# Gated activations and their token sums, 64 bytes further on

## What is computed

```python
def _conv_ffn(x, w_up, conv_w, conv_b, w_down):
    S = x.shape[1]
    h = x @ w_up
    hp = jnp.pad(h, ((0, 0), (CONV_WIDTH - 1, 0), (0, 0)))
    hc = conv_b + sum(conv_w[kk] * hp[:, kk:kk + S] for kk in range(CONV_WIDTH))
    gate = hc[..., :D_FF]
    up = hc[..., D_FF:]
    return (jax.nn.silu(gate) * up) @ w_down
```

## Time and profile before

| | us |
|---|---|
| median of three runs | 2093.48 |
| lowest and highest run | 2093.47, 2095.21 |
| the profiled execution | 2093.4 |
| its span, first to last instruction | 2091.6 |
| TensorE busy | 2083.9 |
| VectorE busy | 1526.0 |
| ScalarE busy | 1226.9 |

### The profile page before, as it was taken

One profiled execution on the slowest core, in us unless ns is written; L12 is line 12 of the kernel. 1 busy time (PEld: TensorE's weight loads), 2 busy tenths in 40 slices (PEclk: granted clock), 3 DMA queues, 4 the chain that ended last, 5 costly groups with the idle time before them and its releaser, 6 DMA issues.

```text
span 2091.6 us, 38907 instructions
## 1 busy us (share of the span) xinstructions
PE 2083.9 (100%) x14540; PEld 1923.5 (92%) x14540; DVE 1526.0 (73%) x2707; ACT 1226.9 (59%) x2223; POOL 2.7 (0%) x12
## 2 busy tenths in 40 slices
PE   9999999999999999999999999999999999999999
PEld 9999889999999998888788888899999999988887
DVE  5767777767676679888756558667766676688888
ACT  5655566555565555666656666566555565555654
POOL 0000000000000000000000000000000000000000
PEclk9999999999999999999999999999999999999999
DMA  9655666555655555556554454745555656555554
GB/s 351 236 170 166 215 214 216 189 193 181 201 199 191 190 181 201 201 182 226 185 171 151 167 187 161 256 157 192 201 192 189 200 180 201 177 204 182 201 201 161
DMA packets 201631, 408.97 MB, mean 196 GB/s; under 512 B 7616, under 2 KB 9152, under 8 KB 200768
## 3 DMA queue, kind: packets, MB, share of 16 engines
q1 hardware_dynamic: 201392, 407.45, 57.4%
q10 hardware_dynamic: 144, 0.26, 0.0%
HBM read 404.53 MB, written 3.15 MB: 195 GB/s over the span
## 4 chain that ended last, share of the span: by engine, by line
PE 98%; DVE 1%; ACT 0%; issue 0%
PE acc L1771 32%; PE acc L1769 32%; PE acc L1770 32%; PE acc L2091 0%; PE acc L1968 0%; PE acc L2065 0%; PE acc L1882 0%; PE acc L1949 0%; PE acc L1934 0%; PE acc L2115 0%; PE acc L1875 0%; PE acc L2123 0%; DVE x_tok L1740 0%; DVE next_w_lo L1058 0%; PE acc L1994 0%; PE acc L1961 0%
## 5 line engine op out<-in xcount | busy, mean ns | idle before, releaser
L1058 DVE TENSOR_TENSOR w_lo<-raw,w_hi 128x512 fp32r<-128x512 f32 x1326 | 878.3, 686 | 410.5 <-ACT w_hi L626 405.9
L626 ACT ACTIVATE w_hi<-raw 128x512 fp32r<-128x512 f32 x1326 | 809.2, 630 | 541.3 <-PE acc L1771 528.1
L1769 PE MATMUL acc<-ffn_xT,w_hi 128*128 128x256 f32 x2920 | 806.9, 276 | 0.0
L1770 PE MATMUL acc<-ffn_xT,w_hi 128*128 128x256 f32 x2920 | 806.0, 276 | 0.0
L1771 PE MATMUL acc<-ffn_xT,w_lo 128*128 128x256 f32 x2920 | 806.0, 276 | 0.0
L1770 PEld LDWEIGHTS acc<-ffn_xT,w_hi 128*128 128x128 f32 x2920 | 548.2, 188 | 0.2
L1769 PEld LDWEIGHTS acc<-ffn_xT,w_hi 128*128 128x128 f32 x2920 | 548.2, 188 | 0.2
L1771 PEld LDWEIGHTS acc<-ffn_xT,w_lo 128*128 128x128 f32 x2920 | 548.1, 188 | 0.0
L1770 PE MATMUL acc<-w_lo,ffn_act 128*128 128x512 f32 (+1 forms) x640 | 234.0, 366 | 0.0
L1769 PE MATMUL acc<-w_hi,ffn_act 128*128 128x512 f32 (+1 forms) x640 | 233.9, 365 | 0.0
L1771 PE MATMUL acc<-w_hi,ffn_act 128*128 128x512 f32 (+1 forms) x640 | 233.7, 365 | 0.0
(11 more groups left out here) (294 smaller groups left out, 1975.9 us busy)
## 6 DMA issues: line engine op xcount, KB each, us to landing
raw<-in_ffn_w_up SPq DMA_DIRECT2D x172, 1024.0 KB, 5.0
raw<-in_ffn_w_down SPq DMA_DIRECT2D x88, 1024.0 KB, 5.1
raw<-in_diff_w_in SPq DMA_DIRECT2D x38, 1024.0 KB, 5.7
raw<-in_w_out SPq DMA_DIRECT2D x32, 1024.0 KB, 5.1
raw<-in_pool_w_in SPq DMA_DIRECT2D x16, 1024.0 KB, 5.2
raw<-in_mem_w_kv SPq DMA_DIRECT2D x12, 1024.0 KB, 12.4
next_from_raw<-in_ffn_w_up SPq DMA_DIRECT2D x4, 1024.0 KB, 9.8
head_first<-in_first SPq DMA_DIRECT2D x5, 768.0 KB, 11.1
```

The lines of the kernel that those rows point to most:

```text
L626: nc.scalar.activation(hi, raw_place(st, c, k, j), ACT.Copy).then_inc(hi_made, 1)
L1058: nc.vector.tensor_tensor(lo, raw_place(st, c, k, j), hi.bitcast(F32), ALU.subtract).then_inc(lo_made, 1)
L1769: pe.matmul(out, w[0], x[0], start=start, stop=False, skip_group_check=True)
L1770: pe.matmul(out, w[0], x[1], start=False, stop=False, skip_group_check=True)
```

## The change

The tile act and the tile pair_x start 64 bytes further on: the margin before them is 32 floats instead of 16, and the large region grows by as much. So everything behind the region moves by 64 bytes too, and so does out_gb, the last layer norm's rows. The tiles up_hi2 and up_lo2 (up_pair_w_hi, up_pair_w_lo) move by 256 bytes. Nothing else moves. Start addresses in the two built programs, modulo 256 bytes (each step from one stationary or moving slice to the next is a multiple of 256 bytes, so a slice has its tile's value):

| tile | before | after |
|---|---|---|
| w_hi, w_lo, next_w_hi, next_w_lo, next_held_w_hi, next_held_w_lo | 192 | 192 |
| ffn_xT, memory_memT, pool_dT | 128 | 128 |
| tokens_xT, x_tok, diff_h_tok, diff_scores, diff_probs, next_tokens | 192 | 192 |
| ffn_act | 192 | 0 |
| pairs_x | 192 | 0 |
| up_pair_w_hi, up_pair_w_lo | 224 | 224 |
| ident, mask, ident_r, mask_r | 32 | 96 |

The diff also writes the counting of the paired pieces in another way (DOWN_PAIRS, sum_count, PAIR_PARTS, granules counted in units in place of pieces). The numbers come out as before: DOWN_PAIRS has paired pieces in chunks 1 to 3 of both layers. In the built programs every engine has the same instructions in the same order with the same waits; only addresses and line numbers differ. The diff, cut to its core:

```diff
-SPLIT_MARGIN, MOVING_MARGIN, STATIONARY_MARGIN = 16, 48, 16
+SPLIT_MARGIN, MOVING_MARGIN, STATIONARY_MARGIN, ACT_MARGIN = 16, 48, 16, 32
...
+DOWN_PAIRS = (((), PAIRED, PAIRED, PAIRED),) * 2
...
-SUMMED, COPIED = 8 + 9 * len(PAIRED), 8 + 3
+PAIR_PARTS = 2 * len(PAIR_SUM)
+COPIED = PAIR_PARTS + 3
...
-        return c > 0 and k in PAIRED
+        return k in self.pairs[c]
...
-    def sum_count(self, l, c, k, step):
-
-        return SUMMED * l + 8 + 3 * ((c - 1) * len(PAIRED) + PAIRED.index(k)) + step
+    def sum_count(self, c, k, step):
+
+        return self.sums_before + PAIR_PARTS + 3 * self.order.index((c, k)) + step
...
-    xT, _, act = region("ffn", [split_x, margin, ("act", [P, FF_T, 2, S], F32R)])
+    act_margin = ("act_margin", [P, ACT_MARGIN], F32)
+    xT, _, act = region("ffn", [split_x, act_margin, ("act", [P, FF_T, 2, S], F32R)])
...
-    apart = ("apart", [P, APART], F32)
+    act_apart = ("apart", [P, APART + MOVING_MARGIN + STATIONARY_MARGIN], F32)
...
-    _, _, _, _, up_hi2, up_lo2 = region("up_pair", [split_x, margin, ("act", [P, FF_T - 2 * PIECE - 5, 2, S], F32R), apart] + pair_split)
+    _, _, _, _, up_hi2, up_lo2 = region("up_pair", [split_x, margin, ("act", [P, FF_T - 2 * PIECE - 5, 2, S], F32R), act_apart] + pair_split)
...
-    _, _, out_gb = region("last", [split_x, margin, ("gb", [P, 2, D], F32)])
-    _, pair_x = region("pairs", [margin, ("x", [P, len(PAIR_SUM), len(PAIRED), 2, 2, P], F32R)])
-    sb("regions", [P, (KT + FF_T) * 2 * S + STATIONARY_MARGIN])
+    _, _, out_gb = region("last", [split_x, act_margin, ("gb", [P, 2, D], F32)])
+    _, pair_x = region("pairs", [act_margin, ("x", [P, len(PAIR_SUM), len(PAIRED), 2, 2, P], F32R)])
+    sb("regions", [P, (KT + FF_T) * 2 * S + ACT_MARGIN])
```

More of the change, by code:

```diff
@@ L141, in total @@
     def total(self):
-        return self.chunks * self.pieces
+        return self.chunks * self.pieces * PIECE
     def units(self, c, k):
@@ L149, in granule @@
     def granule(self, c, k, j):
-        return c * (self.pieces * PIECE) + ((self.first + k) * PIECE + j)
+        return c * (self.pieces * PIECE) + (self.first + k * PIECE + j)
     def loaded(self, c, k):
@@ L179, with __init__ @@
 class PairedStream(Stream):
-    def __init__(self, before, chunks, pieces):
+    def __init__(self, before, chunks, pieces, pairs, sums_before):
         super().__init__(before, chunks, pieces)
+        self.pairs, self.sums_before = pairs, sums_before
+        self.order = [(c, k) for c in range(chunks) for k in pairs[c]]
+        self.sums = sums_before + PAIR_PARTS + 3 * len(self.order)
         starts = [0]
@@ L198, in total @@
     def total(self):
-        return self.starts[-1] // PIECE
+        return self.starts[-1]
     def granule(self, c, k, j):
         at = c * self.pieces + k
-        return self.first * PIECE + (self.starts[at] if at >= 0 else at * PIECE) + j
+        return self.first + (self.starts[at] if at >= 0 else at * PIECE) + j
     def slot_split(self, c, k):
@@ L422, in build @@
     s_up0 = Stream(s_out0, 2 * FF_CHUNKS, 4, apart=HEAD // PIECE)
-    s_down0 = PairedStream(s_up0, 4, FF_T // PIECE)
+    s_down0 = PairedStream(s_up0, 4, FF_T // PIECE, DOWN_PAIRS[0], 0)
     s_diff = Stream(s_down0, DIFF_W // CHUNK, 4, apart=HEAD // PIECE)
@@ L426, in build @@
     s_up1 = Stream(s_out1, 2 * FF_CHUNKS, 4, apart=HEAD // PIECE)
-    s_down1 = PairedStream(s_up1, 4, FF_T // PIECE)
+    s_down1 = PairedStream(s_up1, 4, FF_T // PIECE, DOWN_PAIRS[1], s_down0.sums)
     split_apart = {s_kv: (kv_hi2, kv_lo2, (0, 0, 0)), s_pool_in: (pool_hi2, pool_lo2, (2, 2, 1)),
@@ L633, in hi_unit @@
             if r in SUM_OF:
-                act_e.wait_ge(strassen_summed, st.sum_count(s_down.index(st), c, k, SUM_STEP[r]))
+                act_e.wait_ge(strassen_summed, st.sum_count(c, k, SUM_STEP[r]))
             act_e.wait_ge(granule_used, st.split_free(c, k, i))
@@ L1003, in pair_hi_part @@
             def pair_hi_part(half, step):
-                act_e.wait_ge(strassen_summed, SUMMED * l + 4 * half + step + 1)
+                act_e.wait_ge(strassen_summed, s_down[l].sums_before + 4 * half + step + 1)
                 nc.scalar.activation(pair_x[:, step, 2 * half:2 * half + 2, :, 0, :], pair_place(step), ACT.Copy).then_inc(strassen_copied, 1)
@@ L1017, in _ @@
                     if k == 9:
-                        act_e.wait_ge(granule_used, s_down[l].granule(c, PAIRED[-1], len(UNITS)))
+                        act_e.wait_ge(granule_used, s_down[l].granule(c, s_down[l].pairs[c][-1], len(UNITS)))
                         nc.scalar.activation(gb[:, 0, 0:HALF], acc[:, PAIR_BANKS[0], 0:HALF], ACT.Copy).then_inc(strassen_copied, 1)
@@ L1066, in sum_weights @@
         def sum_weights(st, c, k, step):
-            l = s_down.index(st)
             if step == 0:
@@ L1075, in sum_weights @@
             else:
-                dve.wait_ge(strassen_summed, st.sum_count(l, c, k, step))
+                dve.wait_ge(strassen_summed, st.sum_count(c, k, step))
                 before, block = ((0, 3), (2, 2))[step - 1]
@@ L1088, in lo_piece @@
                 lo_granule(st, c, k, j)
-                if st in s_down and c > 0 and k + 1 in PAIRED and j < 3:
+                if k + 1 < st.pieces and is_paired(st, c, k + 1) and j < 3:
                     sum_weights(st, c, k + 1, j)
@@ L1152, in pair_outputs @@
             v, w = conv[:, 0, 0, 0:HALF], gb[:, 1, 0:HALF]
-            dve.wait_ge(strassen_copied, COPIED * l + 8 + c)
+            dve.wait_ge(strassen_copied, COPIED * l + PAIR_PARTS + c)
             order.done(nc.vector.tensor_tensor(v, gb[:, 0, 0:HALF], acc[:, left, HALF:CHUNK], ALU.add))
@@ L1721, in pair_step @@
                 if step in (3, 6, 8):
-                    dve.wait_ge(strassen_summed, SUMMED * l + 4 * half + sum(at < step for at in (2, 5, 7, 9)))
+                    dve.wait_ge(strassen_summed, s_down[l].sums_before + 4 * half + sum(at < step for at in (2, 5, 7, 9)))
                 if step == 0 and half:
@@ L1815, in paired_piece @@
                     ins = product3(acc[:, b, right * HALF:(right + 1) * HALF], x, (hi[:, ns], lo[:, ns]),
-                                   k == PAIRED[0] and q == 0 and r in STARTS, False)
+                                   k == st.pairs[c][0] and q == 0 and r in STARTS, False)
                 ins.then_inc(granule_used, 1)
```

## The result

| | us |
|---|---|
| before, median of 7 runs (lowest, highest) | 2095.21 (2093.47, 2096.25) |
| changed, median of 7 runs (lowest, highest) | 2101.99 (2100.76, 2103.79) |
| ratio, with its 95% interval | 1.0035 [1.0026, 1.0044] |
| the profiled execution of the changed kernel | 2103.79, a span of 2102.0 |

The kernel became slower by about 7 us. The forecast was 2085.9 in a range from 2075.0 to 2093.9, so the sign and the range were both wrong. The size is that of rival D.

The account below looks back on a forecast made before the run. The prediction took the steps between matmul starts on busy TensorE as the bound. Gains of 4.0 + 2.9 + 0.25 + 0.35 = 7.5 us took 2093.4 to 2085.9 us, range 2075.0 to 2093.9.

Parts of the forecast that it names:

- rival D: Wide matmuls on ffn_act never settle, keeping 232 ns steps: 9.1 us more; 2102.5, or 2095.0 with narrow gains; chance 0.11.
- (4): 512-wide matmuls on ffn_act, 1518: 0 in steady state, 0.35 us gained from settling behind paired pieces.
- (1): Narrow matmuls on pairs_x, 3 x 192: distance becomes 64, each 7 ns shorter, 4.0 us gained.
- (2): 256-wide matmuls on ffn_act, 144 and 288: fall to 276 ns, 2.9 us gained.
- (3): The 36 half-width matmuls on the held weights: 7 ns shorter each, 0.25 us gained.
- (5): Identity behind the regions, moving operand of 260 transposes: taken as 0, bound 1.7 us either way.
- (6): up_pair_w_hi and up_pair_w_lo move by 256 bytes, their distance stays 96: 0.
- (7): VectorE and ScalarE accesses to the moved tiles: 0, neither engine on the chain in the stretches that gain.
- My reading of the cause: Matmul's read and the next weight load's read get in each other's way at distances 0 and 96, not 64.
- A: Narrow matmuls gain, wide ones pay 2.3 ns each, 3.5 us, as at stationary address 128: 2089.4; chance 0.15.
- C: Wide matmuls carry the same 7 ns and lose it too, 10.6 us more gained: 2075.3; chance 0.12.
- B: Nothing changes, since each operand's own address counts, not the distance: 2093.4; chance 0.15.

Follow-up runs that it names:

- e3: Changed kernel with pair_x back at 192 modulo 256 and act left at 0; 2104.25 us, ratio 1.0047 to the kernel before.
- e2: Changed kernel with act back at 192 modulo 256 and pair_x left at 0; 2093.59 us, ratio 0.9994 to the kernel before.
- e4: Changed kernel with w_hi and w_lo moved to 0 modulo 256, act at 0, pair_x at 192; 2144.69 us.
- e10: Changed kernel with act at 192 (distance 0) and pair_x at 128 (distance 192); 2091.12 us, ratio 0.9982 to the kernel before.
- e7: Changed kernel with act at 128 (distance 192) and pair_x at 64 (distance 128), weights at 192; 2097.61 us.
- e13: Changed kernel with the tables and the identity behind the region put back at 32 modulo 256; 2100.36 us.
- e1: Changed kernel run and profiled once more without an edit; 2100.59 us.
- e5: Changed kernel with w_hi and w_lo moved to 0 modulo 256, act and pair_x both at 64; 2154.46 us.

## Why the prediction was wrong, point by point

**What bounds the kernel**: right. TensorE is busy throughout, nobody came late in the down projection (the largest sum of waits was 2.3 us and is 1.9 now, on the same transposes), VectorE's and ScalarE's busy time grew by 0.2 and 0.5 us, and only the steps changed.

**(4), the wide matmuls on ffn_act, is the step that failed.** I took "0 for the steady state" and 0.35 us gained; they cost 9.1 us, 6 ns a step. My reason was that at distance 0 there was "no collision to remove". That was true, and it spoke only of what could be gained: the wide ones were already at their best place. What distance 64 does to wide matmuls no row showed, I said so, and then set the term near zero, with a bound of +3.5 us from the nearest address instead of the 232 ns step, which was in the earlier trace rows. With it the upper bound would have been 9.1 us, as in rival D. e3 shows the loss with act alone moved; e2 shows none with act left in place.

**(1) and (2), the narrow matmuls**: the sign was right and the size wrong. pairs_x brought 1.3 us in place of 4.0, ffn_act 0.8 in place of 2.9. The failed step is "the distance becomes 64, that of the 276 ns rows". Distance 64 has two levels, 276 and 281 ns, and the features chunks of the trace of before nearly always stood on the lower one. The assumption under it, that a distance has one step, is what failed: it fails at 192 as well, where pairs_x stands at 276 in e4 and e10 but the narrow ones on ffn_act at 280 in e7. The first narrow matmul behind a wide run, on which I leaned, was no witness either: it starts with a step of 113 at distance 0 whose followers don't keep it.

**(3), the held narrow ones**: 283 to 277 in the row shown, and 285 to 279 in the mean of their three lines, as forecast.

**(5), (6), (7)**: 0 in the transposes, as taken, and up to 0.5 us lost in features matmuls by the identity's place, for which the prediction had no term (e13). The matmuls on up_pair went from 283 to 280 ns, 0.1 us in all, but in e1, the same kernel, they stand at 283 again, so the change alone doesn't set it.

**My reading of the cause**, two reads in each other's way, is neither shown nor refuted: no run separates the two reads, and the weight loads didn't follow the steps. What is shown is that the wide matmuls' step follows the distance and not the absolute address (e4, e5). Why it does stays open. The Trainium skill, "TensorE: Matmul & The Clock Gate", section "Step-by-step: what each phase is for", says that TensorE reads through two independent ports, and that a weight load takes no read bandwidth from the running matmul. If that were all, none of these runs should differ; e10 and the changed kernel do, by 11 us.

**The rivals.** A and C gave the wide ones the wrong price or sign, B the wrong cause. D named the mechanism, and its price, 1518 x 6 ns, met the measured 9.1 us. It said 2102.5 with no gain in the narrow ones; 2101.99 was measured. That it came within 0.5 us is luck in part: it starts from 2093.4, and against the 2095.21 measured beside it the rise is 6.8 us and not 9.1, since the narrow ones gained the 2.1 us that it left out. I gave it 0.11, because it needed a distance unlike all in the rows. But wide matmuls are three quarters of the down projection's time, and about them I had no row at distance 64: that lack should have weighed more than the neat fit of the narrow ones.

## What to carry to other kernels

Where one tile is an operand of matmuls of two widths, price a move for each width from rows of that width; a row of the narrow kind says nothing of the wide. What counts here is the distance between the two operands modulo 256 bytes, so moving a tile that many loops share (the weights in e4) reaches all of them: some 47 us lost in the features chunks for 4 gained on pairs_x. Give each tile its own margin, and try the few distances on the chip; with a step of 113 ns and one of 120 at stake, no reasoning from the rows of one layout replaced that.

## What the runs showed of the hardware that I hadn't expected

- Wide and narrow matmuls have different best distances: 0 for 512 columns (a step of 227 ns against 229 at 192 and 233 elsewhere), 192 for the 256-column ones on pairs_x (113 against 117 to 120), though not for those on ffn_act (118 in e7).
- At distance 64 a run of narrow matmuls steps by 113 or by 118 ns, with the same instructions at the same addresses. In the down projection the level goes with the last step of the wide run before it: 118 behind 231, 113 behind 236, in all 144 cases of six traces. It is not simply handed through the wide run, as e3 shows. In the features chunks one execution had a stretch at 118 that its repeat had not.
- The wide matmuls on memory_memT, at distance 192 in all kernels but e4 and e5, have medians of 388, 392 and 394 ns in the three lines in some executions and 394 or 395 in all three in others, the changed kernel's among them:

```profile
L1774 PE MATMUL acc<-w_hi,memory_memT x64: 388/394/400, 29.3 to 94.8; 128*128 128x512 f32 x64
```

- TensorE's clock can fall in one execution and not in the next. At the end of layer 0's down projection TensorE waits twice for VectorE, 1.5 and 0.8 us in the profile of before. Behind that stand the first 18 narrow matmuls on held weights. Windows of the kernel before, and of its repeat:

```profile
1010.00:1012.00 2.00, 2.00 (x17) 1.00 0.00 0
```

```profile
1010.00:1012.00 2.00, 2.00 (x11) 0.50 0.00 0
```

  At a granted clock of 1.00 (2.4 GHz) they step by 120 ns, at 0.50 (1.2 GHz) by 213. Before the fall TensorE had been busy for 3.7 of the 6 us from 1004 to 1010 us, in the kernel before and in its repeat alike, and only the repeat's clock fell. The spans are 2091.6 and 2093.1, so about 1.5 us hang on it. That is more than pair_x's whole move in e2, and one reason why such an edit needs many runs of each kernel. The profiles of e2, e4 to e7 and e10 have the dip too, so their single times are not to be read to the microsecond against the others'.
